# Attention heads: values formed for all heads at once, probabilities turned by a product with a diagonal, outputs kept turned

## What is computed

```python
q = (_rms_norm(c_q, q_norm_g) @ w_uq).reshape(bsz, seq, N_HEADS, 64 + 32)      # nope | rope
kv = (ckv @ w_ukv).reshape(bsz, seq, N_HEADS, 64 + 64)                          # keys | values
def attend(blk):
    s = (einsum('bqhd,bkhd->bhqk', qn, k_nope) + einsum('bqhr,bkr->bhqk', qr, k_rope)) * scale
    p = softmax(s, axis=-1)
    return einsum('bhqk,bkhd->bqhd', p, v)
...
mix = concatenate([s, a], axis=-1) @ w_o
x1 = _layer_norm(DEEPNORM_ALPHA * x + mix, ln1_g, ln1_b)
out = _layer_norm(DEEPNORM_ALPHA * x1 + _moe(x1, ...), ln2_g, ln2_b)
```

## Time and profile before

| | us |
|---|---|
| three runs | 1537.32, 1537.36, 1539.86 |
| median | 1537.36 |
| the profiled execution, whole | 1540.41 |
| its span, first to last instruction | 1538.2 |

### The profile page before, as it was taken

The page is one execution under the profiler, slowest core; times in us unless marked ns, Lnnn a source line. Parts: engine busy times, 40 slices in busy tenths (PEclk is TensorE's granted clock), DMA queues, the critical chain, the costliest instruction groups (busy, mean ns, idle before and its releaser), DMA issues.

```text
span 1538.2 us, 17542 instructions
## 1 busy us (share of the span) xinstructions
PE 1418.5 (92%) x5398; PEld 739.5 (48%) x5398; DVE 784.5 (51%) x1420; ACT 373.0 (24%) x745; POOL 613.6 (40%) x590
## 2 busy tenths in 40 slices
PE   7998899999998899999899999999999999999980
PEld 4544666766666445554344444444444444444430
DVE  1385788888888336885333233333333232333325
ACT  1313455555555312220001010100101010100115
POOL 0006455544440001343245554545555554545520
PEclk9999999999999899999999999999999999999995
DMA  9115110011103730124679999999999999999956
GB/s 259 31 41 68 15 20 17 14 19 19 33 17 116 260 137 15 42 80 172 239 256 358 364 368 367 359 359 374 360 373 362 367 361 366 365 365 368 312 124 232
DMA packets 111886, 321.99 MB, mean 209 GB/s; under 512 B 44006, under 2 KB 61054, under 8 KB 86882
## 3 DMA queue, kind: packets, MB, share of 16 engines
q1 hardware_dynamic: 88434, 261.99, 46.0%
q0 software_dynamic: 23408, 59.45, 15.9%
HBM read 276.45 MB, written 51.72 MB: 213 GB/s over the span
## 4 chain that ended last, share of the span: by engine, by line
DMA 40%; PE 5%; issue 4%; DVE 2%; POOLq 1%; ACT 0%; POOL 0%; ACTq 0%; SPq 0%
DMA sum_d<-moe_y,moe_idx 39%; PE moe_p_gu L1713 2%; PE moe_p_s L1749 2%; PE moe_p_y L1733 1%; DVE all_x_sb L1927 1%; DVE all_x_sb L1922 1%; DMA moe_xg<-x_d,moe_idx 1%; DMA all_x_sb<-sum_d 0%; POOLq L1655 0%; POOL moe_xg L1659 0%; POOL sum_d L1670 0%; POOLq L1696 0%; ACT moe_junk L1829 0%; DVE moe_y L1861 0%; POOLq L1656 0%
## 5 line engine op out<-in xcount | busy, mean ns | idle before, releaser
L1844 DVE STREAM_TRANSPOSE moe_xgT<-moe_xg 128x1024 f32<-128x1024 f32 x65 | 132.0, 2030 | 419.1 <-DMA moe_xg<-x_d,moe_idx 419.1
L1659 POOL DMA_INDIRECT moe_xg<-x_d,moe_idx x260 | 264.4, 1017 | 116.0 <-issue 60.5
L1733 PE MATMUL moe_p_y<-mixers_ring_b,moe_hT 128*128 128x512 f32 x520 | 233.9, 592 | 0.9 <-DVE moe_hT L1855 0.9
L1713 PE MATMUL moe_p_gu<-mixers_ring_b,moe_xgT 128*128 128x512 f32 x512 | 225.0, 592 | 0.0
L1670 POOL DMA_INDIRECT sum_d<-moe_y,moe_idx x65 | 105.8, 1627 | 244.5 <-DMA sum_d<-moe_y,moe_idx 207.4
L1781 ACT ACTIVATE moe_sig<-moe_p_gu 128x256 f32<-128x256 f32 x65 | 25.0, 384 | 588.8 <-PE moe_p_gu L1713 588.8
L1733 PEld LDWEIGHTS moe_p_y<-mixers_ring_b,moe_hT 128*128 128x128 f32 x520 | 98.7, 190 | 125.0 <-issue 123.9
L1713 PEld LDWEIGHTS moe_p_gu<-mixers_ring_b,moe_xgT 128*128 128x128 f32 x512 | 95.1, 191 | 107.1 <-issue 107.1
L1239 POOL DMA_INDIRECT slot_d<-all_entry,all_dest_i x48 | 48.5, 1010 | 225.8 <-DVE all_dest_i L1485 213.6
L723 PE MATMUL att_p_s<-latents_kT,att_qT 128*128 128x512 f32 x256 | 123.2, 604 | 1.0 <-ACT att_v L893 0.7
L1713 PE MATMUL moe_p_gu<-mixers_ring_a,moe_xgT 128*128 128x512 f32 x272 | 119.5, 592 | 0.0
(11 more groups left out here) (327 smaller groups left out, 1947.4 us busy)
## 6 DMA issues: line engine op xcount, KB each, us to landing
mixers_ring_b<-in_we_down_dram SPq DMA_DIRECT2D x65, 1024.0 KB, 9.4
mixers_ring_b<-in_we_gate_dram SPq DMA_DIRECT2D x32, 1024.0 KB, 10.3
mixers_ring_b<-in_we_up_dram SPq DMA_DIRECT2D x32, 1024.0 KB, 16.1
mixers_ring_a<-in_we_gate_dram SPq DMA_DIRECT2D x17, 1024.0 KB, 10.1
mixers_ring_a<-in_we_up_dram SPq DMA_DIRECT2D x17, 1024.0 KB, 14.9
mixers_o<-in_we_gate_dram SPq DMA_DIRECT2D x16, 1024.0 KB, 10.1
mixers_o<-in_we_up_dram SPq DMA_DIRECT2D x16, 1024.0 KB, 16.2
all_x_sb<-in_x_dram SPq DMA_DIRECT2D x16, 512.0 KB, 8.8
```

Of the source, the lines that this page charges most:

```text
L1659: nc.gpsimd.indirect_dma_start(xg[:, u, g, :], None, x1_quarters, bass.IndirectOffsetOnAxis(ap=idx[:, c, g:g + 1], axis=0), bounds_check=N ...
L1713: last = nc.tensor.matmul(p_gu[:, u, :], xgT[:, u, kk, :], k.moe_gu[v][:, :, kk * F:(kk + 1) * F], start=(kk == 0), stop=(kk == KD - 1))
L1733: last = nc.tensor.matmul(p_y[:, half * 512:(half + 1) * 512], hT[:, u, kk, :], k.moe_dn[v][:, kk * D + half * 512:kk * D + (half + 1) * 512],
L1844: nc.vector.transpose(xgT[:, u].rearrange("p k (g i) -> p g k i", g=NQ), xg[:, u].rearrange("p g (j k) -> p g k j", k=KD)).then_inc(x_turn ...
```

## The change

The lines of the changed kernel are a few off those before.

1. **Values.** The values of all 8 heads are formed before head 0: for each 128 tokens one product of 512 columns (`all_values`, four rounds of two), copied by ScalarE (`keep_values`) into the places of `k.oT` that outputs will take later, and into `v_last`. `values_of` finds them. The part "v" and its copy are gone from every head. SP loads the values' columns of `w_ukv` once.
2. **Turning.** A probability tile is turned by a plain product whose moving operand is `weigh`, the identity scaled by 1/total in each row, in place of a transpose. VectorE inverts the total of one step (`invert`), ScalarE forms the diagonal from it (`weigh_up`), and TensorE waits for it (`weighed`) before the turn.
3. **Outputs.** They come out already divided and with tokens in columns; ScalarE copies them so, as two half copies, into `k.oT` (`keep_pair`). `turn_pair`, `finish`, and in the mixing stage `turn_o` and `keep_oT` are gone, with their waits.
4. **Parts.** `PARTS = ("k", "q", "q")`: keys behind step 3, queries in steps 4 and 5. The next head's scores wait for the keys and the first query half.
5. **TensorE's heads** are written out, all eight.

The core of the diff:

```diff
-        PARTS = ("q", "q", "k", "v")
+        PARTS = ("k", "q", "q")
+        oT = k.oT[:, :, :].rearrange("p k t -> p (k t)")
...
+        def values_of(hh, u, j):
+            place = v_last if hh == HEADS // 2 - 1 else oT[:, (hh + 1) * SEQ:(hh + 2) * SEQ]
+            return place[:, j * P + u * DV:j * P + (u + 1) * DV]
...
+            def all_values(t):
+                for s in range(2):
+                    place = p_t[:, 4 * s:4 * s + 4, :].rearrange("p j n -> p (j n)")
+                    last = nc.tensor.matmul(place, k.ckvT[:, (t + s) * P:(t + s + 1) * P],
+                                            k.wv[:, :, :].rearrange("p h n -> p (h n)"), start=True, stop=True)
+                last.then_inc(va_done, 1)
...
-                    if t and t % 2 == 0:
-                        turn_pair(pair - 1)
                     if t % 2:
                         pe.wait_ge(pT_kept, n * 2)
+                    pe.wait_ge(weighed, n + 1)
                     for half in range(2):
                         for r in range(4):
                             j = half * 4 + r
-                            last = nc.tensor.transpose(p_t[:, j, :], pr[:, t % 2, j * P:(j + 1) * P], k.ident)
+                            last = nc.tensor.matmul(p_t[:, j, :], pr[:, t % 2, j * P:(j + 1) * P], weigh[:, t % 2, :], start=True, stop=True)
                         last.then_inc(p_turned, 1)
...
-            part(0, 0, 0, banks[0])
+            part(0, 0, 1, banks[0])
             pe.wait_ge(k.cT_read, T)
-            part(0, 0, 1, p_p)
-            part(0, 0, 2, banks[1])
-            part(0, 0, 3, p_o)
+            part(0, 0, 2, p_p)
+            part(0, 0, 0, banks[1])
+            pe.wait_ge(k.wv_in, 16)
+            all_values(0)
             pe.wait_ge(part_kept, NP)
             for t in range(2):
                 scores(0, 0, t)
-            for d in range(2):
-                if d:
-                    pe.wait_ge(vsT_kept, d)
-                turn_vs(0, d)
-            with pe.Fori(0, HEADS // 2 - 1) as hh:
-                for u in range(2):
-                    head(hh, u, True)
-            head(HEADS // 2 - 1, 0, True)
-            head(HEADS // 2 - 1, 1, False)
+            pe.wait_ge(va_kept, 1)
+            all_values(2)
+            turn_vs(0, 0)
+            for t in (4, 6):
+                pe.wait_ge(va_kept, t // 2)
+                all_values(t)
+            pe.wait_ge(vsT_kept, 1)
+            turn_vs(0, 1)
+            pe.wait_ge(va_kept, NPAIR)
+            for h in range(HEADS):
+                head(h // 2, h % 2, h + 1 < HEADS)
...
+            def weigh_up(n, t):
+                act.wait_ge(inverted, n + 1)
+                nc.scalar.activation(weigh[:, t % 2, :], k.ident, ACT.Copy, scale=rtotal[:, t:t + 1]).then_inc(weighed, 1)
...
-            def keep_pair(pair):
+            def keep_pair(hh, u, t, pair):
                 act.wait_ge(o_done, pair + 1)
-                nc.scalar.activation(oh[:, :], p_o[:, 0:P], ACT.Copy).then_inc(oh_kept, 1)
+                for s in range(2):
+                    last = nc.scalar.activation(oT[u * DV:(u + 1) * DV, bass.ds(hh * SEQ + (t - 1 + s) * P, P)], p_o[s * DV:(s + 1) * DV, 0:P], ACT.Copy)
+                last.then_inc(o_read, 1)
...
+            def invert(n, t):
+                dve.wait_ge(probs, n + 1)
+                nc.vector.reciprocal(rtotal[:, t:t + 1], total[:, t:t + 1]).then_inc(inverted, 1)
...
                     if following or t + 2 < T:
                         top(h * T + (t + 2), (t + 2) % T)
+                    if following or t + 1 < T:
+                        invert(h * T + (t + 1), (t + 1) % T)
```

More of the change, by code:

```diff
@@ L730, in part @@
                     for kk in range(2):
-                        last = nc.tensor.matmul(p_p[:, :], wq[:, u, kk, :], k.cqT[:, kk, i * 512:(i + 1) * 512],
+                        last = nc.tensor.matmul(p_p[:, :], wq[:, u, kk, :], k.cqT[:, kk, (i - 1) * 512:i * 512],
                                                 start=(kk == 0), stop=(kk == 1))
-                elif what == "k":
+                else:
                     for half in range(2):
-                        last = nc.tensor.matmul(p_p[half * NOPE:(half + 1) * NOPE, :], wkv[:, u, 0:NOPE],
+                        last = nc.tensor.matmul(p_p[half * NOPE:(half + 1) * NOPE, :], wk[:, u, :],
                                                 k.ckvT[:, half * 512:(half + 1) * 512], start=True, stop=True)
[L737 to L740, removed]
                 last.then_inc(part_done, 1)
+            def all_values(t):
[4 more added lines that the diff above has]
+                last.then_inc(va_done, 1)
             def turn_vs(b, d):
@@ L858, in head @@
                         behind(hh, u, t, following)
-                turn_pair(pair)
             pe.wait_ge(w_in[0], 64)
@@ L945, in head @@
                     if t % 2:
-                        keep_pair(pair)
-                    if following and t in (3, 5):
-                        keep_part(h + 1, 1 - u, 0 if t == 3 else 3)
+                        keep_pair(hh, u, t, pair)
+                    if following and t == 3:
+                        keep_part(h + 1, 1 - u, 0)
                     if following and t == 7:
@@ L955, in _ @@
             act.wait_ge(k.cT_read, T)
-            for i, bank in enumerate((banks[0], p_p, banks[1], p_o)):
-                keep_part(0, 0, i, bank)
-            exponent(0, 0)
-            for d in range(2):
-                keep_vsT(0, d)
+            act.sem_inc(o_read, 1)
+            for place, (i, bank) in enumerate(((1, banks[0]), (2, p_p), (0, banks[1]))):
+                keep_part(0, 0, i, bank, place)
+            act.wait_ge(k.u_out, 16 * 4)
+            keep_values(0)
+            exponent(0, 0)
+            keep_values(2)
+            keep_vsT(0, 0)
+            keep_values(4)
+            weigh_up(0, 0)
+            keep_values(6)
+            keep_vsT(0, 1)
             with act.Fori(0, HEADS // 2 - 1) as hh:
@@ L1252, in _ @@
         def _(pe):
-            def turn_o(t):
-                if t >= 5:
-                    pe.wait_ge(rank_read, t - 4)
-                elif t:
-                    pe.wait_ge(oT_done, t)
-                for q in range(4):
-                    last = nc.tensor.transpose(p_o[:, q * P:(q + 1) * P], k.o[:, t, q * P:(q + 1) * P], k.ident)
-                last.then_inc(o_turned, 1)
             def mix(t):
@@ L1320, in gate @@
                 last.then_inc(z_done, 1)
-            turn_o(0)
-            gate(0)
-            turn_o(1)
-            for m in range(1, 4):
+            for m in range(4):
                 gate(m)
             mix(0)
-            turn_o(2)
             mix(1)
```

102 lines of the change are left out of this document (38 added, 64 removed).

## The result

| | us |
|---|---|
| after, four runs | 1563.36, 1566.93, 1567.54, 1568.76 |
| after, median | 1567.24 |
| before, median of four runs beside them | 1538.61 (1537.32 to 1540.27) |
| ratio | 1.0184, 95% interval 1.0164 to 1.0205 |
| the profiled execution, whole and span | 1566.93, 1565.1 (before: 1540.41, 1538.2) |

1.8% slower. The forecast was 1563 with a range of 1551 to 1579, so the time lies 4 us above it and inside. The added time was forecast as 25.7 us; between the two profiled spans it is 26.9, between the two medians 28.6.

A forecast was written before the change was run, and what follows sets the result against it. TensorE was taken to bound the kernel until the fixed-length expert stage starts. Heads 1 to 6 +24.0, start +1.5, rest of head 0 +2.3, head 7 +1.0, mixing -3.1: +25.7 on 1537.36 gives 1563 us, range 1551 to 1579.

The forecast's parts named there:

- The turn: Turning probabilities on TensorE, each step: eight two-pass products take 1.78 us instead of 0.87, +0.91 a step, +7.3 a head.
- Values: In a full head with one following: the next head's values' product on TensorE goes, -1.84 us.
- Turned-back outputs: In a full head: the pair of outputs is no longer turned back, four saved passes of 0.11 us, -0.4 us.
- Rope wait: In a full head: TensorE's 1.9 us wait for the query's rope rows goes, since keys now come first.
- New wait at the keys' product: Step 3 of a head: keys' product waits for kernels that ScalarE keeps after the diagonal, +0.95 us (bounds 0 and 2).
- A full head: Heads 1 to 6, each with one following: longer turns less savings and waits, +4.0 us each, +24.0 in all.
- Start: Start and steps 0, 1 of head 0: step 2 starts at 162.3 instead of 160.81, +1.5 us (bounds 0, +5.5).
- Head 7: Last head: 40.9 us instead of 40.2 plus a second half copy, +1.0 at full clock; +4.7 at half clock.
- Mixing: Mixing stage: seven of eight groups of output turns save 0.44 us each on TensorE, -3.1 us; the first saves 0.
- the late diagonal: Rival: diagonal held up behind VectorE's and ScalarE's work, 2 to 3 us more lost per head, 1583 us; chance 0.09.
- The rival of one pass: Rival: the product with the diagonal goes as one pass, 512 records, 1512 us; chance 0.05.
- The case of four passes: Rival: eight products with the diagonal take 3.5 us, +109 us beyond the forecast, 1672 us; chance 0.01.

The follow-up runs named there:

- kernel 7: The changed kernel with probabilities turned by one-pass transposes with the identity, without reciprocals, diagonals or their wait, outputs left undivided: 1508.45 us, 0.9811 of before.
- kernel 2: The changed kernel with the turn a two-pass plain product with the identity, without reciprocals, diagonals or their wait, outputs left undivided: 1557.21 us, 1.0126 of before.
- kernel 8: The changed kernel with ScalarE keeping the kernels ahead of the next diagonal in steps 2 and 3 of a head: 1561.51 us, 1.0148 of before.
- kernel 9: The changed kernel with ScalarE's first square of head 7 moved behind the last exponent and last diagonal: 1564.85 us, 1.0171 of before.
- kernel 5: The kernel before with only TensorE's eight heads written out one after another instead of looped over in pairs: 1540.92 us, 1.0015 of before.
- kernels 3: The kernel before with all values formed at once, keys made ahead of queries and heads written out; turn and division as before: 1512.37 us, 0.9826 of before.
- kernel 1: The changed kernel with probabilities turned by one-pass transposes with the identity, the diagonal still formed and awaited but unused: 1538.05 us, 0.9995 of before.

## Why the prediction was right

By heads the experiments lead from one kernel to the other: 44.84, less 1.77 (values), less 1.64 (keys first), less 0.72 (outputs neither divided nor turned back), plus 6.89 (second pass), plus 1.04 (diagonal) is 48.64. Each link is the difference of two neighbouring kernels, so that the sum comes out is no proof; what counts is each link beside its term of the forecast. In another order the last two would be 4.10 for the diagonal and 3.83 for the pass.

- *The turn*, +0.91 us a step, 7.3 a head. The pass count and the 0.111 us of a pass held. In time it is 0.86 a step: a copy that was exposed behind a short half turn is covered by a long one (the waits before the value products are 7.8 us in kernel 7, 5.2 in kernel 2).
- *Values*, -1.84: -1.77. *Turned-back outputs*, -0.4: -0.72, though that link also holds the division. *Rope wait*, -1.9: -1.64, for 0.2 us stays. *New wait at the keys' product*, +0.95: +1.0 by kernel 8, from the order named in the text. *A full head*, +4.0: +3.80.
- *Start*, step 2 of head 0 at 162.3: 162.13. That is in part luck, for this mark moves without the change: kernel 9, with the same start, has it at 159.92, and kernel 5, with the start of the kernel before, at 154.38 where that one has 160.81. *Rest of head 0*: 0.4 us more than forecast.
- *Head 7*, +1.0: **mis-sized, +4.05**. The step that failed is "turn 1.8, a wait of 1.1 for the copies and the diagonal, turn 1.8". The wait is 2.33, because I left out the square of 1.06 us that ScalarE does ahead of the exponent, and took 0.28 for the diagonal's 0.39; behind that wait the turn ran at the lower clock, 3.60 in place of 1.8. With the square moved the wait is 1.26 and the turn 2.02 (kernel 9); without the diagonal the wait is still 2.05 (kernel 2). From its start to the gate product head 7 has 45.84 us before, so the forecast was 46.8; it has 47.98 in kernel 2 and 48.38 in kernel 9, both at full clock, and 49.89 in the change. So the square is paid wherever it stands, for 1.1 to 1.5 us with what little else was mis-sized, and the lower clock makes up most of the rest. The condition "This takes full clock to the end" failed, and the stated upper bound of +4.7 was nearly the truth. The rule of the Trainium skill that I named there ("TensorE: Matmul & The Clock Gate", Part 4: PE-mode transpose, on transposes not counting as activity) gave no safety here: all turns in this stretch were plain products, and the clock fell. The runs do not decide the rule, for kernel 2, with plain products too, kept 1.00 after 2.05 us of waiting.
- *First gate product*: +1.4, not foreseen, and not shown to come from the change. The kernel before with only its heads written out has it 9.56 us long as well, with the loop 8.17; it varies from 8.11 to 10.18 over the eleven profiles.
- *Mixing*, -3.1: -3.1, and the same between kernels 3 and 7. *Expert stage*, 0: -2.3, but over the eleven profiles, none of which touches that stage, it is 793.3 to 799.0 us long. It is scatter; the text also had TensorE through with the shared expert at 733.81, while its last product, 64 records, only begins at 739.94, but the forecast does not hang on that. With this scatter the sum of 25.7 against 26.9 is nearer than its parts by luck.

Of the rivals, the late diagonal did not come, but only since turns are long; the text saw the reason ("TensorE's step grew and VectorE's did not"). The rival of one pass was decided by the records, as the text said it would be, but it was wrong in its price: 1512 would have been 1538 (kernel 1), since it took the cost of the turns away and left the waits as counted. The case of four passes is refuted by 1024 records and 1.78 us. It is the one to which the Trainium skill, "TensorE: Matmul & The Clock Gate", Terms, would lead with its fourfold transpose mode.

Open: what the turned outputs alone are worth in the heads, for no kernel keeps them turned and divides behind.

## What to carry to other kernels

Count passes, not instructions: for f32 in these traces a turn by transpose leaves one record and the same turn as a plain product two (0.87 and 1.78 us for eight), so folding a scaling into the turn costs as much as the turn itself. The Trainium skill gives the rule in "Perfetto Trace Analysis", Transposes ("Ensure logical transpose operations use transpose, as opposed to a standard matmul"); kernels 2 and 7, 48.8 us apart, agree. Take a change apart before judging it: the values and keys alone give 0.983 of the time before, and the turn by a product with a diagonal gave all of it back and as much again. And when a long operation is made short, ask which chain it had covered: 52 us of passes, by the expectation, gave back 29.

## What was not expected of the hardware

The clock can fall in one head after a wait that does no harm in another. In the kernel with values only, the wait of about 1.85 us ahead of the second queries' product comes in seven heads; in heads 3, 4 and 6 the next products are slow. Head 3, in TensorE's order of time and in the stretches:

```profile
302.59 3.11 PE L737 MATMUL att_p_p<-latents_cqT,latents_wq 128*128 128x512 f32 x4 [1.85 <-DVE att_qT L993]
305.49 2.49 PE L729 MATMUL att_p_s<-latents_kT,att_qT 128*128 128x512 f32 x4
```

```profile
292.00:302.00 10.00, 8.26 (x67) 5.14 (x65) 9.64 (x13) 6.30 (x18) 6.65 (x6) 1.00 0.01 2
302.00:308.00 6.00, 5.41 (x10) 2.34 (x11) 4.01 (x9) 1.68 (x3) 0.00 (x0) 0.72 0.24 44
```

The granted clock was 0.72 for those 6 us, and each of the three heads took 44.75 us in place of 43.07. That is 5 us in the profiled execution of 1528.82; it may be why this kernel came out at 1527 and not at 1524, but the other three executions have no profile. The kernel before, with waits of 0.9 to 1.8 us there, had none of it in its profiled execution. With its heads written out it had it in head 5, after a wait of 1.85, and the kernel with one pass and the diagonal in head 4, after waits of 1.70 and 2.27 us: 46.5 in place of 44.8. So in these three profiles waits of 1.6 to 2.3 us on TensorE (one of 3.5) cost their own length and, in 5 of 21 heads, 1.7 us more; why in these heads, the runs do not say.
